# Layer norms centred early on the mean of their first half, and first units that begin with the high parts

## The chip, the cores and the metric

The kernel runs on one core of a Trainium2 chip. The metric is the device time of one launch in microseconds (us), as the median of several runs. All numbers of the profile come from one profiled execution.

## What is computed

The reference runs two transformer blocks after each other on one sequence of 256 tokens of width 1024, in fp32. The first block has two layers: sparse attention and gated linear attention as mixers, each followed by a layer norm, then a squared-relu MLP followed by a layer norm. These four norms are what the change is about:

```python
def layer_norm(x, g, b):
    xf = x.astype(jnp.float32)
    mu = jnp.mean(xf, axis=-1, keepdims=True)
    var = jnp.mean(jnp.square(xf - mu), axis=-1, keepdims=True)
    return ((xf - mu) * lax.rsqrt(var + LN_EPS) * g + b).astype(x.dtype)

# first_block, layer i
h = layer_norm(DN_ALPHA * h + mix, ln_mix_g[i], ln_mix_b[i])                          # ln0, ln2
h = layer_norm(DN_ALPHA * h + squared_relu_mlp(h, mlp_w_up[i], mlp_w_down[i]), ...)   # ln1, ln3
```

The second block normalises by rms (pre_mix, post_mix, pre_x, post_x, pre_ffn, post_ffn, mem), and has its own mixers, cross attention and a gated MLP.

## The kernel before

Activations stand transposed: 8 blocks of 128 features by 256 tokens, in `h` (the residual stream) and `z`. Weights are read as 183 "units" of 128 x 2048 elements, in one fixed order, by DMAs from the SP queue into four buffers `raw`. Each unit is split in two: ScalarE copies the high part to `whi` (`high_part`), VectorE subtracts to get the low part `wlo` (`low_part`). Both run three units ahead of the products (AHEAD = 3). Activations are split the same way into `xh` and `xl`, in four chunks of two blocks, with the semaphores `split_hi` and `split_lo`. A product of a unit is three matmuls (`three`): high by high, high weight by low activation, low weight by high activation. A unit is 48 matmuls of 128 x 256 into one of four PSUM banks `lin`. Each use of a bank is a "job" with a number; `plan()` writes out the order of the jobs by hand, TensorE follows it, and ScalarE and VectorE each have an order of their own, joined by semaphores only.

- Narrow units `ao` and `go` (4 each, before ln0 and ln2): each makes two blocks. VectorE's `residual` does for each: `low_part`, z = ALPHA * h + product (L1546), and two additions to `zsum` (`add_up`, L1538).
- Down units `dn` (8 for each half of an MLP): each makes one block. The second half adds to `z` (L1728) and to `zsum`. Up and down units run in loops of two times four.
- `layer_norm`: TensorE multiplies `zsum` by a matrix of ones (L580), so every partition has the sum over features. VectorE subtracts 1/1024 of it from `z` in four operations (`center`, L1461). ScalarE squares each chunk (L1023), VectorE adds the two blocks of chunks 2 and 3 (L1452), TensorE sums the squares over features (`token_sum`, L544), ScalarE takes the root (`deviation`, L1036), VectorE the inverse (L1454), TensorE spreads it over the partitions (`spread`, L567). VectorE scales (L1476), ScalarE makes `xh` (L1055), VectorE makes `xl` (L1490) and writes `h` (L1506).
- `unit_first` is the first unit after a norm: for each chunk it waits for `split_lo` and does all three kinds of product of that chunk, for both output blocks.
- `keep_warm(n)` puts n products of the identity with itself (L537) into TensorE's queue; nobody reads them. `norm` has 6 (or 0) of them before the square sum, 4 before the spreading and 11 after it, `layer_norm` has 5 before the mean.
- A product in full fp32 (L537, L544, L567, L580) is shown as two records in the profile.

Of the kernel before, what the change touches and what calls it, by code (L numbers as in the profile page):

```python
# [17 lines left out]
P = 128  # L18
S = 256
D = 1024  # L20
DB = D // P
RING = 4
# [45 lines left out]
def plan():  # L68
# [18 lines left out]

    add("ik"); units("iq", 2); add("iw"); add("rope", 0); add("rope", 1); add("rope", 2)
# [10 lines left out]
    units("ao", 4); norm("ln0", True)  # L99
    for layer in range(2):  # L100
        for half in range(2):
            units(f"up{layer}{half}", 8); units(f"dn{layer}{half}", 8)
        norm(f"ln{2 * layer + 1}", True)
        if layer == 0:
# [11 lines left out]
            units("go", 4); norm("ln2", True)  # L116
# [14 lines left out]
    for u in range(COUNT["fd"]):  # L131
# [11 lines left out]
          ("inv", 1), ("rot", 1), ("norot", 1), ("ln_eps", 1), ("rms_eps", 1), ("one", 1), ("zero", 1)]  # L143
# [6 lines left out]
def shape_constants():  # L150
# [32 lines left out]
    put("one", np.ones((P, 1)))  # L183
    return c

def build(nc, units_d, x_d, mem_d, pos_d, vec_d, const_d, narrow_a_d, narrow_b_d, narrow_f_d, w_a2_d, b_fgt_d, lam_d, out_d):
# [4 lines left out]
    with ctx:  # L192
# [36 lines left out]
        squares_of = pr + lg  # L229

# [65 lines left out]
        z_summed, centered, squared, normed = sem("z_summed"), sem("centered"), sem("squared"), sem("normed")  # L296
        paired, scaled, inv_ready = sem("paired"), sem("scaled"), sem("inv_ready")
# [23 lines left out]
        CENTERED = counts([(e, 3) for e in ("ln0", "ln1", "ln2", "ln3", "conv")])  # L321
        SQUARED = counts([("ln0", 4), ("ln1", 4), ("ln2", 4), ("ln3", 4), ("pre_mix", 4), ("conv", 2), ("mem", 4),
                          ("post_mix", 4), ("pre_x", 4), ("post_x", 4), ("pre_ffn", 4), ("post_ffn", 4)])

        PAIRS = {"ln0": (2, 3), "ln1": (2, 3), "ln2": (2, 3), "ln3": (2, 3), "conv": (0, 1), "mem": range(4), "post_mix": range(4),
# [5 lines left out]
        SUMMED = {"ln0": 0, "ln1": 8, "ln2": 16, "ln3": 24}  # L331
# [119 lines left out]
        def _(pe):  # L451
# [29 lines left out]
            def unit_first(u, j, event, g=None):  # L481
# [9 lines left out]
                last.then_inc(job_done, 1)  # L491

            def unit_down(u, j, first, g=None):
# [3 lines left out]
                for k in range(UT):  # L497
                    if first is not None and k % 2 == 0:
                        pe.wait_ge(flo, first + k // 2 + 1)
# [77 lines left out]
            def layer_norm(name):  # L577
# [3 lines left out]
                norm(name)  # L581
# [154 lines left out]
            ups("ao", "ao")  # L736
# [3 lines left out]
            def mlp(layer):  # L740
                for half in range(2):
# [7 lines left out]
                    with pe.Fori(0, 2) as g:  # L749
                        for i in range(RING):  # L750
# [1450 lines left out]
```

## Time and profile before

| | |
|---|---|
| runs | 1348.9, 1351.1, 1351.09 us; median 1351.09 |
| the profiled execution | 1351.66 us, its span 1349.9 us |
| TensorE matmul (PE) | 1295.1 us, 96% of the span |
| VectorE (DVE) | 899.4 us, 67% |
| ScalarE (ACT) | 643.9 us, 48% |
| chain that ended last | PE 78%, DVE 13%, ACT 3%, issue 3%, POOL 2%, DMA 1% |
| mean granted TensorE clock | 0.992 |

The busy share of PE is an upper bound on useful work: it contains the idle products of `keep_warm`, and matmuls overlap in the records. The chain of waits says for each moment what the end of the program hung on.

### The profile page before, as it was taken

Reading aid. Unit: us, or ns where it says so; the run is one execution under the profiler, and the core shown is the slowest. Engines: PE = TensorE matmul, PEld = TensorE weight load, DVE = VectorE, ACT = ScalarE, POOL = GpSimd, SP = SyncE. Lnnn points to the kernel's source line nnn. Section 1 sums busy time; section 2 is a strip of 40 time slices with the busy share of each in tenths; the row PEclk is TensorE's granted clock in tenths of the full one; section 3 lists DMA queues with packets and bytes.
Section 4 is the critical chain, followed back from the end, with each engine's and each line's share of the span. In section 5 each row is a group of like instructions: output and inputs, shape, how many; then the busy total and the mean of one; then the engine's idle time right before and its main releaser. Section 6 shows DMA issues by size and latency. Waiting matters only on the chain.

```text
span 1349.9 us, 25141 instructions
## 1 busy us (share of the span) xinstructions
PE 1295.1 (96%) x10650; PEld 1251.7 (93%) x10650; DVE 899.4 (67%) x1373; ACT 643.9 (48%) x838; POOL 46.3 (3%) x40
## 2 busy tenths in 40 slices
PE   9989999999997999999999999999799999999997
PEld 8869999999886999999999998889798989999997
DVE  6875764565568576556664369879766564899843
ACT  5463553543463435335345453544445455777631
POOL 0561000000000000000000000000000000000000
PEclk9999999999998999999999999999999999999999
DMA  9223355554332135555524543334355241455530
GB/s 363 97 95 103 112 192 187 181 193 156 128 125 80 56 117 187 190 184 187 187 70 186 183 161 100 120 126 142 139 179 196 94 157 63 142 176 183 185 126 32
DMA packets 28505, 198.41 MB, mean 147 GB/s; under 512 B 3440, under 2 KB 3952, under 8 KB 4736
## 3 DMA queue, kind: packets, MB, share of 16 engines
q1 hardware_dynamic: 27792, 195.83, 40.5%
q10 hardware_dynamic: 624, 1.31, 0.3%
q8 instruction: 66, 1.08, 0.3%
q14 instruction: 23, 0.19, 0.0%
HBM read 196.08 MB, written 1.05 MB: 146 GB/s over the span
## 4 chain that ended last, share of the span: by engine, by line
PE 78%; DVE 13%; ACT 3%; issue 3%; POOL 2%; DMA 1%; SPq 0%; DVEq 0%; ACTq 0%
PE lin L462 23%; PE lin L464 22%; PE lin L463 22%; DVE conv L1910 3%; DVE wlo L1436 3%; PE lin L544 3%; PE att L537 2%; ACT whi L997 1%; PE lin L567 1%; DMA narrow_a<-narrow_a_dram 1%; PE att L623 1%; POOL pr L447 1%; DVE qk L1777 1%; DVE z L1527 0%; POOL lg L447 0%
## 5 line engine op out<-in xcount | busy, mean ns | idle before, releaser
L462 PE MATMUL lin<-xh,whi 128*128 128x256 f32 x1936 | 555.7, 287 | 3.9 <-DVE xl L1490 2.1
L1436 DVE TENSOR_TENSOR wlo<-raw,whi 128x2048 fp32r<-128x2048 f32 x179 | 409.6, 2291 | 211.6 <-ACT whi L997 210.5
L463 PE MATMUL lin<-xl,whi 128*128 128x256 f32 x1936 | 549.7, 284 | 0.0
L464 PE MATMUL lin<-xh,wlo 128*128 128x256 f32 x1936 | 549.4, 284 | 0.0
L997 ACT ACTIVATE whi<-raw 128x2048 fp32r<-128x2048 f32 x183 | 348.5, 1906 | 180.4 <-PE lin L464 171.0
L462 PEld LDWEIGHTS lin<-xh,whi 128*128 128x128 f32 x1936 | 373.4, 193 | 9.1 <-issue 5.7
L463 PEld LDWEIGHTS lin<-xl,whi 128*128 128x128 f32 x1936 | 373.5, 193 | 0.6 <-issue 0.5
L464 PEld LDWEIGHTS lin<-xh,wlo 128*128 128x128 f32 x1936 | 373.2, 193 | 0.0
L462 PE MATMUL lin<-fh,whi 128*128 128x256 f32 x512 | 143.4, 280 | 0.0
L464 PE MATMUL lin<-fh,wlo 128*128 128x256 f32 x512 | 142.9, 279 | 0.0
L463 PE MATMUL lin<-fl,whi 128*128 128x256 f32 x512 | 142.9, 279 | 0.0
L464 PEld LDWEIGHTS lin<-fh,wlo 128*128 128x128 f32 x512 | 96.3, 188 | 0.0
L462 PEld LDWEIGHTS lin<-fh,whi 128*128 128x128 f32 x512 | 96.1, 188 | 0.0
L463 PEld LDWEIGHTS lin<-fl,whi 128*128 128x128 f32 x512 | 95.8, 187 | 0.0
L537 PE MATMUL att<-consts 128*128 128x128 f32 x512 | 64.5, 277 | 0.0
L537 PEld LDWEIGHTS att<-consts 128*128 128x128 f32 x512 | 60.6, 192 | 1.9 <-issue 1.7
L1910 DVE SCALAR_TENSOR_TENSOR conv<-upad,vec,conv 128x256 f32<-128x256 f32 x120 | 58.1, 484 | 3.9
L462 PE MATMUL lin<-whi,xh 128*128 128x256 f32 x176 | 50.5, 287 | 0.0
L463 PE MATMUL lin<-wlo,xh 128*128 128x256 f32 x176 | 49.8, 283 | 0.0
L464 PE MATMUL lin<-whi,xl 128*128 128x256 f32 x176 | 49.8, 283 | 0.0
L462 PE MATMUL lin<-gh,whi 128*128 128x256 f32 x176 | 49.3, 280 | 0.0
L464 PE MATMUL lin<-gh,wlo 128*128 128x256 f32 x176 | 49.1, 279 | 0.0
(335 smaller groups left out, 1621.3 us busy)
## 6 DMA issues: line engine op xcount, KB each, us to landing
raw<-units_dram SPq DMA_DIRECT2D x183, 1024.0 KB, 4.8
h<-x_dram SPq DMA_DIRECT2D x1, 1024.0 KB, 6.9
memT<-mem_dram ACTq DMA_DIRECT2D x1, 1024.0 KB, 4.8
out_dram<-h SPq DMA_DIRECT2D x4, 256.0 KB, 2.0
consts<-consts_dram SPq DMA_DIRECT2D x1, 864.0 KB, 15.5
narrow_a<-narrow_a_dram SPq DMA_DIRECT2D x1, 544.0 KB, 9.0
vec<-vectors_dram SPq DMA_DIRECT2D x1, 245.5 KB, 17.7
posi<-pos_dram SPq DMA_DIRECT2D x1, 128.0 KB, 8.8
```

The costliest lines, as they stand in the source:

```text
L447: last = nc.gpsimd.tensor_scalar(x, x, ainv[:, n, m:m + 1], None, ALU.mult)
L462: mm(out, w[0], a[0], start=first, stop=False)
L463: mm(out, w[0], a[1], start=False, stop=False)
L464: return mm(out, w[1], a[0], start=False, stop=last)
L537: mm(att[0][:, 0:P], ident, ident, start=True, stop=True)
L544: ins = mm(flat[:, (col + t) * width:(col + t + 1) * width], block[:, t * P:(t + 1) * P], ones[:, 0:width], start=first and t == 0, stop=l ...
L567: last = mm(o[:, n, t * P:(t + 1) * P], inv[:, col:col + 1].broadcast_to([P, P]), ident, start=True, stop=True)
L623: last = mm(o, v, pT[u % 2][:, n, :], start=b == 0, stop=b == att_keys(u, m) // P - 1)
L997: f(whi[u % RING][:], raw[u % RING][:], ACT.Copy).then_inc(hi_ready, 1)
L1436: v.tensor_tensor(wlo[u % RING][:], raw[u % RING][:], whi[u % RING][:].bitcast(f32), ALU.subtract).then_inc(lo_ready, 1)
L1777: ins = v.tensor_tensor(part[0], part[1], part[2], ALU.mult)
L1910: ins = v.scalar_tensor_tensor(out=conv[:, b, :], in0=x, scalar=w, in1=conv[:, b, :], op0=ALU.mult, op1=ALU.add)
```

## The change

- The job order gets a product `ln_shift` for each layer norm. It multiplies `zsum` by ones when only half of the blocks have been added, within unit 2 of `ao`/`go` or unit 4 of the last down units (`near_sum`).
- `near_shift` on VectorE then subtracts this mean (twice the half sum over 1024) from all eight blocks: from `z` where it is there, from `h` (divided by ALPHA) or the half-made `z` where the product is still to come. It corrects `zsum` by the same.
- ScalarE squares the shifted blocks as they come (`near_squares`), VectorE adds the squares block by block (`add_squares`).
- After the last block the product of `zsum` with ones gives the mean that is left. ScalarE squares one row of it (`shsq`), and TensorE adds -1 times this to the one remaining sum of squares. VectorE subtracts the mean left from `z` and then takes the inverse.
- The last narrow unit is written as two jobs of one block each (`two_jobs`). The second-half down units are written out instead of looped.
- `unit_first` does the products with the high activations of chunks 0 and 1 first, and those with the low ones one chunk later.
- Idle products: 2 instead of 4 before the spreading in every `norm`; in a layer norm 1 and 2 around the small product and 8 after the spreading.

```diff
@@ plan @@
+    def narrow_units(name, ln):
+        add(name, 0, name); add(name, 1, name); add(ln + "_shift"); add(name, 2, name); add(name, 3, name, 2)
+        norm(ln, True)
...
@@ tensor @@
-                for c in range(4):
+                def with_high(c):
+                    pe.wait_ge(split_hi, SPLIT[event] + c + 1)
+                    for m in range(2):
+                        for k in (2 * c, 2 * c + 1):
+                            w = tile(u, m * DB + k)
+                            mm(o[:, m, :], w[0], xh[:, k, :], start=m == k == 0, stop=False)
+                            mm(o[:, m, :], w[1], xh[:, k, :], start=False, stop=False)
+
+                def with_low(c):
                     have(event, c + 1)
                     for m in range(2):
                         for k in (2 * c, 2 * c + 1):
-                            last = three(o[:, m, :], tile(u, m * DB + k), (xh[:, k, :], xl[:, k, :]), m == k == 0, m == 1 and k == DB - 1)
+                            last = mm(o[:, m, :], tile(u, m * DB + k)[0], xl[:, k, :], start=False, stop=m == 1 and k == DB - 1)
+                    return last
+
+                with_high(0)
+                for c in range(1, 4):
+                    with_high(c)
+                    with_low(c - 1)
+                with_low(3).then_inc(job_done, 1)
...
+            def near_sum(ln):
+                pe.wait_ge(z_summed, SUMMED[ln] + 4)
+                mm(bank(JOB[ln + "_shift", 0])[:, 0, :], ones, zsum[:], start=True, stop=True).then_inc(job_done, 1)
...
             def norm(name, idle=6):
                 keep_warm(idle)
                 square_sum(name)
-                keep_warm(4)
+                keep_warm(2)
                 spread(name)
                 keep_warm(11)
...
                 mm(bank(JOB[name + "_mean", 0])[:, 0, :], ones, zsum[:], start=True, stop=True).then_inc(job_done, 1)
-                norm(name)
+                pe.wait_ge(near_added, ADDED[name] + 5)
+                o = bank(JOB[name + "_sq", 0])
+                token_sum(o, 0, squares_of[0][:, 0, :], True, False)
+                keep_warm(1)
+                pe.wait_ge(shift_squared, LN[name] + 1)
+                flat = o[:].rearrange("p a s -> p (a s)")
+                for t in range(2):
+                    last = mm(flat[:, t * P:t * P + 8], shsq[:, t * P:(t + 1) * P], const("neg")[0:1, :], start=False, stop=t == 1)
+                last.then_inc(job_done, 1)
+                keep_warm(2)
+                spread(name)
+                keep_warm(8)
...
@@ scalar @@
             def layer_norm(name, event, bias):
-                squares(name, z, is_centered(name))
+                j = JOB[name + "_mean", 0]
+                filled(act, j)
+                f(shsq, lin[j % RING][0:1, 0, :], ACT.Square, scale=D ** -0.5).then_inc(shift_squared, 1)
                 deviation(name, D, eps_ln)
...
@@ vector @@
-                center(name, z, D)
+                j = JOB[name + "_mean", 0]
+                p = psum(j)
+                dve.wait_ge(shift_squared, LN[name] + 1)
+                for c in range(4):
+                    ins = v.scalar_tensor_tensor(out=two(z, c), in0=over(p[:, 0, :]), scalar=-1.0 / D, in1=two(z, c), op0=ALU.mult, op1=ALU.add)
+                    if c == 3:
+                        read_out(ins, j)
+                    elif c == 2:
+                        link(ins)
                 inverse(name)
-                link(v.memset(zsum[:], 0.0))
-                is_centered(name)
+                evacuated(dve, j)
...
+            def near_shift(ln, src, alpha):
+                j = JOB[ln + "_shift", 0]
+                p = psum(j)
+                for n, c in enumerate((2, 3, 0, 1)):
+                    v.scalar_tensor_tensor(out=two(z, c), in0=over(p[:, 0, :]), scalar=-2.0 / D / (alpha if c >= 2 else 1.0),
+                                           in1=two(src if c >= 2 else z, c), op0=ALU.mult, op1=ALU.add).then_inc(shifted, 1)
+                read_out(v.scalar_tensor_tensor(out=zsum[:], in0=p[:, 0, :], scalar=-8.0 / D, in1=zsum[:], op0=ALU.mult, op1=ALU.add), j)
+                evacuated(dve, j)
+                dve.wait_ge(shifted, 4 * LN[ln] + 4)
...
+            def residual(name, ln):
+                sq = squares_of
                 for i in range(4):
                     low_part(U0[name] + i + AHEAD)
                     j = JOB[name, i]
+                    if i == 2:
+                        near_shift(ln, h, ALPHA)
+                    elif i == 3:
+                        add_squares(ln, 1, 2, sq[0][:], sq[1][:])
+                        add_squares(ln, 2, 3, sq[0][:], sq[2][:])
+                        add_squares(ln, 3, 3, sq[0][:, 0, :], sq[0][:, 1, :])
+                    if i < 3:
+                        ...
+                    else:
+                        for m in (6, 7):
+                            j = JOB[name, 3] + m - 6
+                            read_out(v.scalar_tensor_tensor(out=z[:, m, :], in0=z[:, m, :], scalar=ALPHA, in1=psum(j)[:, 0, :], op0=ALU.mult, op1=ALU.add), j)
+                            evacuated(dve, j)
+                            add_up(m, SUMMED[ln] + m + 1)
+                            add_squares(ln, 4 + m - 6, 4 + m - 6, sq[0][:, 0, :], sq[3][:, m - 6, :])
...
@@ vector, second-half down units @@
+                        ln, sq = f"ln{2 * layer + 1}", squares_of
+                        for i in range(8):
+                            low_part(U0[dn] + i + AHEAD)
                             j = JOB[dn, i]
+                            if i == 4:
+                                near_shift(ln, z, 1.0)
+                            elif i == 6:
+                                add_squares(ln, 1, 2, sq[0][:], sq[1][:])
+                            elif i == 7:
+                                add_squares(ln, 2, 4, sq[0][:], sq[2][:])
+                                add_squares(ln, 3, 5, sq[0][:, 0, :], sq[0][:, 1, :])
+                                add_squares(ln, 4, 5, sq[0][:, 0, :], sq[3][:, 0, :])
+                            read_out(v.tensor_tensor(z[:, i, :], z[:, i, :], psum(j)[:, 0, :], ALU.add), j)
+                            evacuated(dve, j)
+                            add_up(i, SUMMED[ln] + i + 1)
+                        add_squares(ln, 5, 6, sq[0][:, 0, :], sq[3][:, 1, :])
```

## Rows read from the trace of the kernel before

**Rows 1.** The page, part 1: busy us (share of the span) and instructions.
```profile
PE 1295.1 (96%) x10650; PEld 1251.7 (93%) x10650; DVE 899.4 (67%) x1373; ACT 643.9 (48%) x838; POOL 46.3 (3%) x40
```

**Rows 2.** The chain of waits around ln0: start us, length us, what.
```profile
134.05 0.70 DVE z L1546
...
135.72 0.71 PE lin L580 x2
...
142.42 0.88 DVE z L1476 x2
...
144.27 0.89 DVE xl L1490 x2
```

**Rows 3.** Timeline of VectorE, 128 to 155 us: start, length, engine, line, operation, count.
```profile
128.29 0.69 DVE L1546 SCALAR_TENSOR_TENSOR z<-h,lin 128x512 f32<-128x512 f32 x1 [1.39 <-PE lin L464]
129.01 0.89 DVE L1538 TENSOR_TENSOR zsum<-zsum,z 128x256 f32<-128x256 f32 x2
130.37 2.29 DVE L1436 TENSOR_TENSOR wlo<-raw,whi 128x2048 fp32r<-128x2048 f32 x1 [0.47 <-ACT whi L997]
...
136.52 2.48 DVE L1461 SCALAR_TENSOR_TENSOR z<-lin,z 128x512 f32<-128x512 f32 x4 [0.86 <-PE lin L580]
...
141.28 0.17 DVE L1454 RECIPROCAL inv<-dev 128x2 f32<-128x2 f32 x1 [1.15 <-ACT dev L1036]
...
148.49 0.88 DVE L1490 SCALAR_TENSOR_TENSOR xl<-z,vec,xh 128x256 fp32r<-128x256 f32 x2 [0.19 <-ACT xh L1055]
...
153.92 0.68 DVE L1715 TENSOR_TENSOR sqr<-relu 128x512 f32<-128x512 f32 x1
```

**Rows 4.** Timeline of ScalarE at ln0.
```profile
139.69 1.28 ACT L1036 ACT_TABLE_LOAD   x1
140.98 0.26 ACT L1036 ACTIVATE dev<-lin,consts 128x2 f32<-128x2 f32 x1
143.33 1.71 ACT L1055 ACTIVATE xh<-z,vec 128x256 fp32r<-128x256 f32 x4 [2.09 <-DVE z L1476]
...
147.55 0.91 ACT L1055 ACTIVATE xh<-z,vec 128x256 fp32r<-128x256 f32 x2 [0.67 <-DVE z L1476]
...
151.54 0.60 ACT L1167 ACTIVATE relu<-lin 128x512 f32<-128x512 f32 x1 [1.27 <-PE lin L464]
```

**Rows 5.** Timeline of TensorE: full fp32 products of 256 columns, and idle products.
```profile
11.95 3.65 PE L683 MATMUL lin<-h,narrow_a 128*72 128x256 f32 x16 [1.23 <-DMA narrow_a<-narrow_a_dram]
...
142.11 2.62 PE L537 MATMUL att<-consts 128*128 128x128 f32 x22
```

**Rows 6.** Timeline of VectorE at ln1: last residual, and inverse.
```profile
328.52 0.42 DVE L1728 TENSOR_TENSOR z<-z,lin 128x256 f32 x1 [1.53 <-PE lin L464]
...
334.94 0.17 DVE L1454 RECIPROCAL inv<-dev 128x2 f32<-128x2 f32 x1 [1.14 <-ACT dev L1036]
```

**Rows 7.** The chain of waits: idle products around pre_mix, the DMA of memT.
```profile
689.22 3.80 PE att L537 x34
...
697.93 2.46 PE att L537 x22
...
1030.09 4.80 DMA memT<-mem_dram
```

**Rows 8.** Waits of TensorE: us in total, times, longest.
```profile
PE lin L462 <- DVE xl L1446: 1.1, 3, 0.5
```

**Rows 9.** Timeline of TensorE: two starts after idle time, in brackets.
```profile
395.21 1.57 PE L785 MATMUL lin<-qk 128*64 128x64 f32 x32 [3.18 <-DVE qk L1777]
...
960.34 1.97 PE L905 MATMUL lin<-conv,consts 128*128 128x256 f32 x8 [2.91 <-DVE conv L1910]
```

**Rows 10.** Windows: busy us (x) by engine, granted clock, DMA share, GB/s.
```profile
396.00:397.00 1.00, 1.00 (x17) 0.88 (x14) 0.35 (x1) 0.61 (x1) 0.00 (x0) 0.50 1.01 418
...
420.00:430.00 10.00, 6.80 (x102) 6.50 (x103) 9.79 (x15) 4.77 (x4) 0.00 (x0) 0.51 0.22 93
...
961.00:962.00 1.00, 1.00 (x8) 0.87 (x6) 1.00 (x1) 0.00 (x0) 0.00 (x0) 1.00 0.00 0
```

More of the change, by code:

```diff
@@ L98, in plan @@
         add("scores", p, banks=2)
-    units("ao", 4); norm("ln0", True)
+    narrow_units("ao", "ln0")
     for layer in range(2):
         for half in range(2):
-            units(f"up{layer}{half}", 8); units(f"dn{layer}{half}", 8)
+            units(f"up{layer}{half}", 8)
+            if half == 0:
+                units(f"dn{layer}0", 8)
+        for i in range(8):
+            if i == 4:
+                add(f"ln{2 * layer + 1}_shift")
+            add(f"dn{layer}1", i, f"dn{layer}1")
         norm(f"ln{2 * layer + 1}", True)
@@ L115, in plan @@
             add("gla_sq"); add("gla_rstd", 0); add("gla_rstd", 1)
-            units("go", 4); norm("ln2", True)
+            narrow_units("go", "ln2")
     norm("pre_mix")
@@ L183, in shape_constants @@
     put("one", np.ones((P, 1)))
+    put("neg", -np.ones((P, 8)))
     return c
@@ L320, in build @@
         SCALED = counts([(e, 3) for e in ("ln0", "ln1", "ln2", "ln3", "pre_mix", "mem", "pre_x", "pre_ffn")])
-        CENTERED = counts([(e, 3) for e in ("ln0", "ln1", "ln2", "ln3", "conv")])
-        SQUARED = counts([("ln0", 4), ("ln1", 4), ("ln2", 4), ("ln3", 4), ("pre_mix", 4), ("conv", 2), ("mem", 4),
+        CENTERED = counts([("conv", 1)])
+        LN = {"ln0": 0, "ln1": 1, "ln2": 2, "ln3": 3}
+        SQUARED = counts([("pre_mix", 4), ("conv", 2), ("mem", 4),
                           ("post_mix", 4), ("pre_x", 4), ("post_x", 4), ("pre_ffn", 4), ("post_ffn", 4)])
-        PAIRS = {"ln0": (2, 3), "ln1": (2, 3), "ln2": (2, 3), "ln3": (2, 3), "conv": (0, 1), "mem": range(4), "post_mix": range(4),
+        PAIRS = {"conv": (0, 1), "mem": range(4), "post_mix": range(4),
                  "post_x": range(4), "post_ffn": range(4)}
@@ L330, in build @@
                                        "post_x", "pre_ffn", "post_ffn")])
-        SUMMED = {"ln0": 0, "ln1": 8, "ln2": 16, "ln3": 24}
+        SUMMED = {ln: 8 * i for ln, i in LN.items()}
+        NEAR = counts([("ln0", 5), ("ln1", 6), ("ln2", 5), ("ln3", 6)])
+        ADDED = {ln: 5 * i for ln, i in LN.items()}
         def per(n, g, step):
@@ L735, in _ @@
             keep_warm(9)
-            ups("ao", "ao")
+            narrow_units("ao", "ln0", "ao")
             layer_norm("ln0")
@@ L842, in _ @@
             keep_warm(9)
-            ups("go", "go")
+            narrow_units("go", "ln2", "go")
             layer_norm("ln2")
@@ L1508, in layer_norm @@
                         ins.then_inc(normed, 1)
+                link(v.memset(zsum[:], 0.0))
                 dve.wait_ge(normed, NORMED[name] + 4)
```

114 lines of the change are left out of this document (82 added, 32 removed).

## The prediction

> **What bounds the kernel now.** I read the page first: the matrix engine is busy for 96% of the span [rows 1], so time is lost only in the few stretches where it has no product to do. The chain of waits shows such a stretch at each of the four layer norms. In the first [rows 2] the last product unit ends at 134.05 us and the next unit's first product waits for the low part written from 144.27 to 145.16. All that lies between is work of a norm: residual and sum, the mean by a product with ones, centring, squares, their sum, root, inverse, spreading, scaling, splitting. The timelines of VectorE and ScalarE put each step in its place [rows 3, 4]. So the norm's chain sets the time there, and whatever is moved under the last units is free only as long as VectorE has room beside them. A busy digit for the matrix engine proves nothing in these stretches: idle products on the identity fill them.
>
> **The room.** A narrow unit (ao, go) lasts 134.05 - 128.29 = 5.76 us [rows 2, 3]. VectorE's share of one is residual 0.69, two sums 0.89, one low part 2.29 [rows 3]: 3.9 of 5.76. A down unit has half as wide a residual and one sum: about 3.15 of 5.65.
>
> **Added product.** The mean of the first half is one product of 256 columns in full precision. Sixteen records of that shape took 3.65 us [rows 5], two take 0.46. It stands within a unit that keeps the matrix engine busy, so it is on the path: +0.46 for each norm, 1.8 in all.
>
> **ln0 and ln2 (after ao and go).** I count from the end of unit 1, t = 0 (122.53 by the 5.76 pitch). Unit 1's residual and sums end at 1.6, its low part lies at 2.1 to 4.4. The shift waits for it. It is four operations like centring, 2.48 us for four [rows 3], and one of 256 columns (0.42, as a sum): 4.4 to 7.3. Unit 2 ends at 6.2, its residual and sums run from 7.4 to 9.0, so VectorE is already a microsecond late. The low part goes to 11.3, then come two additions of 512 (0.68 each by the row of sqr [rows 3]) and one of 256: 13.2. Unit 3 ends at 11.95, so what is late next is VectorE. Two half residuals, two sums and one addition of squares, 0.42 to 0.45 each, follow: the sum is ready at 15.6. ScalarE's squares of the early blocks start at 8.2, behind the high part, and are never last. Before, the mean product stood at 135.72, t = 13.2: it comes 2.4 us later. From there the new chain is short. Mean product to reader is 136.52 - 135.72 = 0.80 [rows 2, 3]; the square of one row of 256 on ScalarE is between 0.26 (two columns) and 0.49 (256 columns with a pointer bias, half of the two in 0.91) [rows 4], I take 0.40 as nearest to the latter; then VectorE corrects z in 2.48, and the inverse is queued behind that, although the root is ready sooner. Inverse at 15.6 + 0.8 + 0.4 + 0.05 + 2.5 = 19.4, against 141.28, which is 18.75. So this part of the change makes ln0 and ln2 later by 0.6 each, the added product included. It takes the squares and most of their sums off the path and puts VectorE's own queue in their place.
>
> The table load of ln0 (1.28 us, 139.69 to 140.97) lay under the square sum, and the root began 0.01 us after it [rows 4]. Now it comes after the square of the row: 16.8 + 1.28 + 0.26 = 18.4, still a microsecond before VectorE is free at 19.4, so it costs nothing. If the cover were gone it would cost up to 1.28, once: ln1, ln2 and ln3 need no load. The Trainium skill (ScalarE: Activation LUTs, "What ACT_TABLE_LOAD costs") counts some 1380 ns of draining beside the 1283 ns of the load; by that ln0 alone would be another 0.4 us later and the total below 0.4 smaller. This case's trace shows the load at that length and no drain behind it.
>
> **ln1 and ln3 (after the down units).** The shift falls into unit 4 of 8: low part until 4.1 after the end of unit 3, shift and sum until 7.1, where unit 4 ends at 6.1. One microsecond late, but unit 5 has the room to give it back. In unit 7 the low part ends 4.1 after unit 6, then 0.68 + 0.43 + 0.43 of additions: 5.8 against the unit's 5.65. From the end t = 0 of the last unit: residual at 0.15, sum ready at 1.05, mean product at 1.1 (before, some 0.97), row read at 1.9, squared by 2.3, corrected until 4.8, inverse at 4.8. The last block's square and its addition end at 1.6, and its two token sums and the two small products follow before 2.7: not last. Before, the inverse began at 334.94 - 328.52 = 6.4 [rows 6]. Gain 1.6, less the 0.46 of the added product: 1.15. The shorter fill before spreading (below) makes it 1.25 each.
>
> **High products lead.** Scaling starts at S = 142.42; ScalarE's first two high blocks end at S + 1.8 and S + 2.6, the fourth at S + 6.0 and the third one pitch of 1.58 earlier [rows 4]; the low part of the first ends at S + 2.74, that of the last at S + 6.95 [rows 2, 3]. Before, the first product stood at S + 2.88 and ScalarE read the unit at 151.54, S + 9.1 [rows 4]. Now: 16 products with high parts from S + 1.85 (eight for a block, the product spacing being 5.76 / 48 = 0.12; 1.92 for blocks 0 and 1 together), low ones of block 0 until S + 4.2, block 2 from S + 4.5, block 3 from S + 6.1 to 7.1, the last low products until S + 8.0, read at S + 8.35. Gain 0.75 where the unit waits for its parts: ln0, ln1, ln2. At the other first units the data or the fill is ahead of the products: after pre_mix, for one, 22 fill records are the step before it [rows 7], and the first high part is ready before they end. There it is worth nothing. Products waited for plain low parts 1.1 us in all [rows 8], 0.9 of it at "out"; behind "out" ScalarE's squares of memT wait for a DMA of 4.80 us from 1030.09 [rows 7] that does not come sooner, and the matrix engine waits for those, so I count nothing there; the other end is 0.8.
>
> **Fill.** One idle product is two records; 22 records take 2.62 us or less in a row, about 0.23 for each product [rows 5]. Three fewer after each layer norm matter only where they gate: between ln3 and pre_mix 34 records (3.80 us) stand on the chain before a square sum whose first squares are there sooner [rows 7]. Six records fewer give 0.67. With the 1.25 that is 1.9 for ln3; the squares of pre_mix shift with it. Two fewer products between square sum and spreading (0.45 of cover) uncover only what the inverse needs, some 0.1 at each of the eight norms that have it (ln0 to ln3 too).
>
> **Other edits at nothing.** The memset of zsum moves behind the eight operations on h, under the first unit. The down units of the second half are written out instead of looped: narrow units, which are written out too, keep the matrix engine just as full as the loops do [rows 1]. Low parts and raw loads are a microsecond later in units 2 and 3, but they are three units ahead; that cover is about 17 us.
>
> **The sum**, against the profiled execution (1351.66; its span is 1349.9 and 1.8 lies around it): ln0 and ln2 +0.6 - 0.1 - 0.75 = -0.25 each; ln1 -1.25 - 0.75 = -2.0; ln3 -1.9; pre_mix, post_x, pre_ffn, post_ffn together -0.4. Total -4.8: 1346.9. The runs' median is 1351.09, 0.6 below that execution, so I forecast 1346.3. What follows ln1 is partly bound by VectorE, but all of it starts from the norm and moves with it.
>
> **The rivals.**
> (a) VectorE is later at the down units' end than I count (each wait between dependent additions costs a few hundredths in the rows and could cost 0.2; an ACT square could come last). For it: the budget there is 0.15 us over. Against it: unit 5 and 6 have slack. Then ln1 and ln3 gain about 0.3 each less the product: the total is -2.4, 1348.7.
> (b) The matrix engine's clock falls. In ln0 and ln2 fill ends at t = 13.1, the engine idles until 15.6, works some 2 us, idles again 17.7 to 19.7. In this trace 3.18 us without work (to 395.21) were followed by a granted clock of 0.50, while 2.91 us (to 960.34) left it at 1.00 [rows 9, 10]. Each of the new gaps is shorter than either of those, but there are two close together, and no row shows that. The low level (1.2 GHz) after the former lasted about 3.3 us, and half of that is lost: 1.65 at each of two norms, -4.8 + 3.3 = -1.5, 1349.6. The Trainium skill (TensorE: Matmul & The Clock Gate, "HAM oscillation — how this bites in real kernels") warns of just such bursts between waits; the trace agrees for the longer gap and not for the shorter.
> (c) Slower than before: the same, but lasting. From 420 to 430 the clock stood at 0.51 for ten microseconds in which the engine also worked [rows 10]. If the low level reached through the first unit after ln0 and ln2, it would cost half of 9 us at each: -4.8 + 9 = +4.2, 1355.3. It decides from a loss of 7.5 us in all. Against it: whole first units follow at once.
> (d) The change does better: the correction's tail is hidden, the 0.8 of "out" passes: -6.5, 1344.6.
>
> **How the numbers follow.** Forecast 0.52 (1345.3 to 1348.3), (a) 0.13, (b) 0.15, (c) 0.10, (d) 0.10. A measurement of this kernel can tell about 0.2% (2.7 us) from no change, so faster means below 1348.4: forecast and (d), a little of (a): 0.63 in all (0.52 + 0.10 + 0.01). Within: the rest of (a) and most of (b), 0.26. Slower: (c) and a mix of (b) and (c), 0.11. The range leaves out (c) and the far end of (d): 1344.0 to 1351.0.
>
> **What would show it.** VectorE's timeline: after ao and go the product of zsum starts 3.7 us after unit 3 ends (1.7 before, [rows 2]); the inverse follows the fourth correction at once in all four norms. In ln1 and ln3 the inverse begins 4.8 us after the last down unit; if it is above 5.5, (a). The first product after a norm starts 1.85 us after scaling starts. The granted clock near 142 and 495: below 1.00 is (b). The forecast is wrong above all if the inverse does not wait for the correction, or if the two narrow norms lose more than 0.6 each.

## The result: slower, where a gain of 4.8 us was forecast

The changed kernel takes 1354.23 us (median of 12 runs, 1352.66 to 1355.36) beside 1351.10 for the kernel before (12 runs on the same chip). The ratio is 1.0026, with a 95% interval of 1.0017 to 1.0034: 3.1 to 3.5 us slower, and outside the range that was given (1344.0 to 1351.0). The profiled execution took 1354.28, its span is 1352.5 and its mean granted clock 0.985 (before: 0.992).

First the norms, since the forecast was about them. VectorE at ln0 after the change (start, length, engine, line, operation, count, idle time before), the counterpart of [rows 3]:

```profile
123.94 0.69 DVE L1689 SCALAR_TENSOR_TENSOR z<-h,lin 128x512 f32<-128x512 f32 x1 [1.39 <-PE lin L481]
...
128.23 1.28 DVE L1664 SCALAR_TENSOR_TENSOR z<-lin,h 128x512 f32<-128x512 f32 x2
129.42 1.28 DVE L1664 SCALAR_TENSOR_TENSOR z<-lin,z 128x512 f32<-128x512 f32 x2
130.62 0.41 DVE L1666 SCALAR_TENSOR_TENSOR zsum<-lin,zsum 128x256 f32<-128x256 f32 x1
...
138.71 0.42 DVE L1655 TENSOR_TENSOR zsum<-zsum,z 128x256 f32<-128x256 f32 x1
...
140.43 2.61 DVE L1606 SCALAR_TENSOR_TENSOR z<-lin,z 128x512 f32<-128x512 f32 x4 [0.77 <-ACT pT L1135]
142.96 0.16 DVE L1563 RECIPROCAL inv<-dev 128x2 f32<-128x2 f32 x1
144.00 1.66 DVE L1585 SCALAR_TENSOR_TENSOR z<-z,vec,lin 128x256 f32<-128x256 f32 x4 [0.89 <-PE lin L626]
```

The residual of unit 1 begins at 123.94. The shift (L1664), the late sum and the correction (L1606) stand in the order foretold, and the inverse (L1563) follows the correction with no idle time in brackets. It is 19.0 us behind 123.94; 19.4 was forecast from the unit's end. ScalarE and TensorE at the same norm, the counterparts of [rows 4, 2]:

```profile
139.93 0.37 ACT L1135 ACTIVATE pT<-lin 1x256 f32<-1x256 f32 x1 [0.80 <-PE lin L639]
140.32 1.28 ACT L1110 ACT_TABLE_LOAD   x1
141.61 0.26 ACT L1110 ACTIVATE dev<-lin,consts 128x2 f32<-128x2 f32 x1
...
152.31 0.60 ACT L1265 ACTIVATE relu<-lin 128x512 f32<-128x512 f32 x1 [0.46 <-PE lin L516]
```

```profile
139.19 0.70 PE L639 MATMUL lin<-zsum,consts 128*128 128x256 f32 x2 [2.23 <-DVE zsum L1655]
...
143.17 0.71 PE L626 MATMUL lin<-consts,inv 128*128 128x128 f32 x4 [1.34 <-DVE inv L1563]
143.72 1.95 PE L596 MATMUL att<-consts 128*128 128x128 f32 x16
145.96 0.36 PE L509 MATMUL lin<-xh,whi 128*128 128x256 f32 x1 [0.29 <-ACT xh L1141]
```

The table load ends at 141.60, the root begins at 141.61, and VectorE is not free before 142.96. The first product stands 1.96 us behind the start of scaling (forecast 1.85, before 2.88), the first unit is read 8.31 behind it (forecast 8.35, before 9.1). At ln1, beside [rows 6]:

```profile
331.46 0.42 DVE L1890 TENSOR_TENSOR z<-z,lin 128x256 f32<-128x256 f32 x1
...
336.16 0.15 DVE L1563 RECIPROCAL inv<-dev 128x2 f32<-128x2 f32 x1
337.54 1.66 DVE L1585 SCALAR_TENSOR_TENSOR z<-z,vec,lin 128x256 f32<-128x256 f32 x4 [1.22 <-PE lin L626]
```

The inverse comes 4.7 us behind the residual of the last unit instead of 6.4. So the norms did what they were meant to do. But that residual stood at 328.52 before [rows 6] and stands at 331.46 now: 2.9 us were lost ahead of ln1. The clock took 1.4 of them by a stretch at its lower level at 70 to 74 us, ahead of all changed code and behind a wait of 1.66 us that the kernel before has too (1.65, its clock stays at 1.00). The added products of ln0 and ln1 took 0.4 each, and the first unit after ln0 gave 0.9 back. The high parts of the down units show what else it was: some 1.6 us. ScalarE copies one for each unit, so two starts lie one unit apart where the matrix engine has no wait. Before, then after:

```profile
300.13 1.92 ACT L997 ACTIVATE whi<-raw 128x2048 fp32r<-128x2048 f32 x1 [3.74 <-PE lin L464]
305.79 1.92 ACT L997 ACTIVATE whi<-raw 128x2048 fp32r<-128x2048 f32 x1 [3.73 <-PE lin L464]
```

```profile
296.36 1.92 ACT L1071 ACTIVATE whi<-raw 128x2048 fp32r<-128x2048 f32 x1 [3.84 <-PE lin L481]
302.12 1.92 ACT L1071 ACTIVATE whi<-raw 128x2048 fp32r<-128x2048 f32 x1 [3.84 <-PE lin L481]
307.88 1.92 ACT L1071 ACTIVATE whi<-raw 128x2048 fp32r<-128x2048 f32 x1 [3.84 <-PE lin L481]
```

A down unit lasted 5.66 us and lasts 5.76, with the same 48 products, the clock at its upper level and no wait within it; the step is the same in the down units of the first half, whose code the change does not alter. 32 such units cost 32 x 0.105 = 3.4 us. The eleven longer units of the last feed-forward's second half (fd, which stream gh) lose 0.12 to 0.15 each, as 7.77 to 7.92, some 1.4 in all. That makes 4.8 us, as much as the norms were to give.

The second place is late in the program, where the matrix engine waits for the squares of memT (norm "mem", within the units of "out"). Before, then after, with the first full microsecond of products behind the wait:

```profile
1041.71 1.13 PE L544 MATMUL lin<-consts,pr 128*128 128x128 f32 x8 [1.98 <-DVE pr L1452]
1042.00:1043.00 1.00, 1.00 (x11) 1.00 (x10) 0.57 (x2) 0.00 (x0) 0.00 (x0) 1.00 0.66 115
```

```profile
1040.82 2.05 PE L603 MATMUL lin<-consts,pr 128*128 128x128 f32 x8 [3.09 <-DVE pr L1561]
1041.00:1042.00 1.00, 1.00 (x5) 1.00 (x6) 0.67 (x3) 0.00 (x0) 0.00 (x0) 0.50 0.45 98
```

In each pair the first line is from the timeline and the second from the windows. Up to there the profile of the changed kernel was ahead: the high part number 133 (the units are counted from 0) starts at 983.78 us against 985.07 before, in spite of the longer down units. Behind the longer wait its clock stands at 0.50 from 1040 to 1046, and the two steps between high parts that span the place take 15.66 us (1036.11 to 1051.77) instead of 13.01 (1037.01 to 1050.02): 2.65 us. The experiments take both places up.

### The profile page after: what moved, and what is told of

The parts are those of the page before. It is cut to its first block, busy times and chain, and to the rows that moved or that the text cites. A ratio compares the mean times of both kernels' runs of the same rounds, so it can differ in the third digit from the quotient of the medians.

```text
span 1352.5 us, 24795 instructions
## 1 busy us (share of the span) xinstructions
PE 1292.8 (96%) x10498; PEld 1247.5 (92%) x10498; DVE 917.0 (68%) x1407; ACT 644.3 (48%) x848; POOL 46.3 (3%) x40
## 4 chain that ended last, share of the span: by engine, by line
PE 79%; DVE 12%; ACT 3%; issue 3%; POOL 2%; DMA 1%; SPq 0%; DVEq 0%; ACTq 0%
PE lin L479 21%; PE lin L480 21%; PE lin L481 21%; DVE wlo L1545 2%; DVE conv L2071 2%; PE att L596 2%; PE lin L603 2%; PE lin L509 2%; PE lin L516 2%; PE lin L510 2%; ACT whi L1071 1%; PE lin L626 1%; PE att L693 1%; DVE z L1606 1%; DMA narrow_a<-narrow_a_dram 1%
## 5 line engine op out<-in xcount | busy, mean ns | idle before, releaser
L479 PE MATMUL lin<-xh,whi 128*128 128x256 f32 x1728 | 495.9, 287 | 0.8 <-POOL wlo L453 0.7
L480 PE MATMUL lin<-xl,whi 128*128 128x256 f32 x1728 | 490.9, 284 | 0.0
L481 PE MATMUL lin<-xh,wlo 128*128 128x256 f32 x1728 | 490.7, 284 | 0.0
L479 PEld LDWEIGHTS lin<-xh,whi 128*128 128x128 f32 x1728 | 334.0, 193 | 4.3 <-issue 2.8
L480 PEld LDWEIGHTS lin<-xl,whi 128*128 128x128 f32 x1728 | 334.0, 193 | 0.7 <-issue 0.5
L481 PEld LDWEIGHTS lin<-xh,wlo 128*128 128x128 f32 x1728 | 333.6, 193 | 0.0
L596 PE MATMUL att<-consts 128*128 128x128 f32 x416 | 56.7, 287 | 0.0
L596 PEld LDWEIGHTS att<-consts 128*128 128x128 f32 x416 | 52.2, 200 | 1.8 <-issue 1.7
L509 PE MATMUL lin<-xh,whi 128*128 128x256 f32 x208 | 52.9, 289 | 0.6 <-ACT xh L1141 0.6
L510 PE MATMUL lin<-xh,wlo 128*128 128x256 f32 x208 | 51.5, 283 | 0.0
```

Source lines behind the costliest of these rows:

```text
L479: mm(out, w[0], a[0], start=first, stop=False)
L480: mm(out, w[0], a[1], start=False, stop=False)
L481: return mm(out, w[1], a[0], start=False, stop=last)
L509: mm(o[:, m, :], w[0], xh[:, k, :], start=m == k == 0, stop=False)
L510: mm(o[:, m, :], w[1], xh[:, k, :], start=False, stop=False)
L596: mm(att[0][:, 0:P], ident, ident, start=True, stop=True)
```

## The experiments

```diff
-  ..., ("zero", 1), ("neg", 8)]
+  ..., ("zero", 1), ("neg", 1)]
...
-    put("neg", -np.ones((P, 8)))
+    put("neg", -np.ones((P, 1)))
...
-  last = mm(..., const("neg")[0:1, :], start=False, stop=t == 1)
+  last = mm(..., const("neg")[0:1, :].broadcast_to([1, 8]), start=False, stop=t == 1)
```

> The changed kernel with one edit: the constant of -1 takes one column instead of eight (read by a broadcast), so every buffer after the constants, fh, fl, gh and gl among them, has the address it had before the change (32 bytes lower). Theory L (the shift of 32 bytes slows the down products, 0.1177 to 0.120 us each over 32 down units and 11 units of the last product): 4 to 5 us faster than the changed kernel, so 1349 to 1350.5, ratio to before about 0.999. Theory C (the loss is the low clock after ln1 and ln3 alone): the down products stay at 0.120 us, the time stays at 1354, ratio 1.0025.

e2 and e3 are the kernel before with unused columns at the end of the constants.

```diff
-  ..., ("one", 1), ("zero", 1)]
+  ..., ("one", 1), ("zero", 1), ("pad", 8)]
```

> The kernel before with eight unused columns behind the constants, so that all buffers after them lie 32 bytes higher, as in the changed kernel; no instruction differs. Theory L: down products at 0.120 us, 4 to 5 us slower than before, ratio 1.003 to 1.004. Theory C: ratio 1.000.

> The kernel before with sixteen unused columns behind the constants: all buffers after them lie 64 bytes higher. If what counts is whether fh and fl start at a multiple of 64 bytes (before: yes, shifted by 32: no), ratio 1.000 and down products at 0.1177 us. If it counts that they are offset by 64 from a multiple of 128 (before: yes; here they are at a multiple of 128, as xh and xl are, whose products take 0.120 us), ratio 1.003 to 1.004. Theory C: ratio 1.000.

Measured: e1 1347.78 us, ratio 0.9979 (0.9971 to 0.9988). e2 1355.54, 1.0041 (1.0028 to 1.0054). e3, with 16 columns, 1354.67, 1.0027 (1.0018 to 1.0035). e1 came out 1.2 us below the range expected for it, e2 and e3 at most 0.0003 beside theirs. High parts of down units in e1, then e2, then e3:

```profile
294.33 1.92 ACT L1071 ACTIVATE whi<-raw 128x2048 fp32r<-128x2048 f32 x1 [3.73 <-PE lin L481]
299.99 1.92 ACT L1071 ACTIVATE whi<-raw 128x2048 fp32r<-128x2048 f32 x1 [3.74 <-PE lin L481]
305.64 1.92 ACT L1071 ACTIVATE whi<-raw 128x2048 fp32r<-128x2048 f32 x1 [3.73 <-PE lin L481]
```

```profile
295.76 1.92 ACT L997 ACTIVATE whi<-raw 128x2048 fp32r<-128x2048 f32 x1 [3.84 <-PE lin L464]
301.52 1.92 ACT L997 ACTIVATE whi<-raw 128x2048 fp32r<-128x2048 f32 x1 [3.84 <-PE lin L464]
```

```profile
294.95 1.92 ACT L997 ACTIVATE whi<-raw 128x2048 fp32r<-128x2048 f32 x1 [3.77 <-PE lin L464]
300.65 1.92 ACT L997 ACTIVATE whi<-raw 128x2048 fp32r<-128x2048 f32 x1 [3.78 <-PE lin L464]
```

e1 has 5.66 again and the changed kernel's gain comes to light: 3.3 us below before. e2 computes and issues exactly what the kernel before does, only 32 bytes of nothing are added, and it is 4.4 us slower with the changed kernel's 5.76. So the shift of addresses is a cause, shown from both sides. e3 (`fh` at 0) has 5.70, between the two; its units explain about 2 of its 3.6 us, and the rest has no row.

**2. Which address counts.** In the kernel before, units that stream xh (at 0, as the weights are) take 5.76, those that stream fh (at 64) 5.66. Either xh's own place is bad or its distance from the weights. e4 is the kernel before with 64 bytes ahead of xh, and 64 more ahead of consts, so that xh goes to 64 and the weights and fh stay at 0 and 64. e5 is e1 with the same. e11 leaves xh at 0 and fh at 64 and moves the weights to 64.

```diff
+  sbuf("pad0", [P, 16])
   xh = sbuf("xh", [P, DB, S], f32r)
   xl = sbuf("xl", [P, DB, S], f32r)
+  sbuf("pad1", [P, 16])
   consts = sbuf("consts", [P, NC])
```

> The kernel before with an unused 64 bytes ahead of xh and 64 more ahead of the constants: xh and xl are then offset by 64 from a multiple of 128, as fh and fl are in the kernel before, and stay so. If this offset is what makes the down products take 0.1177 us, the up and narrow products fall from 0.120 to 0.1177 us: some 5300 to 6300 products, 12 to 14 us faster, ratio 0.990. If the two spacings come from the kind of unit (up and down) and not from addresses, ratio 1.000.

> The changed kernel with the constant of -1 in one column and, besides, 64 unused bytes ahead of xh and 64 ahead of the constants: fh, fl, xh and xl all offset by 64 from a multiple of 128. If the gain of the edits (0.9979 with the old addresses) and the gain of the addresses (0.9851 in the kernel before) add up, ratio 0.983 and about 1328 us. If the shorter units leave VectorE less room beside ao and go, so that the sums end later after the last unit, one or two us of that are lost: 0.985.

> The kernel before with the weights' two parts whi and wlo offset by 64 bytes from a multiple of 128, xh, xl at a multiple and fh, fl offset by 64, as before. If the spacing of the products goes by the address of the streamed activations alone, nothing changes: up units 5.76 us, down units 5.65, ratio 1.000. If it goes by the distance between weights and activations, the two swap: up units 5.65 us and down units 5.76, ratio 0.990 to 0.993.

Measured: e4 1331.30 us (1326.35 to 1337.42), ratio 0.9851 (0.9828 to 0.9874). e5 1333.89, 0.9871 (0.9856 to 0.9886). e11 1340.39, 0.9917 (0.9903 to 0.9930). High parts of up units, which stream xh: before, e4, e11.

```profile
250.61 1.90 ACT L997 ACTIVATE whi<-raw 128x2048 fp32r<-128x2048 f32 x1
256.36 1.90 ACT L997 ACTIVATE whi<-raw 128x2048 fp32r<-128x2048 f32 x1
```

```profile
243.31 1.90 ACT L999 ACTIVATE whi<-raw 128x2048 fp32r<-128x2048 f32 x1
248.97 1.90 ACT L999 ACTIVATE whi<-raw 128x2048 fp32r<-128x2048 f32 x1
```

```profile
249.51 1.90 ACT L999 ACTIVATE whi<-raw 128x2048 fp32r<-128x2048 f32 x1
255.16 1.91 ACT L999 ACTIVATE whi<-raw 128x2048 fp32r<-128x2048 f32 x1
```

The length of a unit (mean of many starts, units with a wait or an added product left out) and the offsets modulo 128:

| kernel | weights | xh | up unit | fh | down unit |
|---|---|---|---|---|---|
| before, e1 | 0 | 0 | 5.76 | 64 | 5.655 |
| after, e2 | 0 | 0 | 5.76 | 96 | 5.76 |
| e3 | 0 | 0 | 5.76 | 0 | 5.70 |
| e4 | 0 | 64 | 5.653 | 64 | 5.655 |
| e11 | 64 | 0 | 5.654 | 64 | 5.695 |
| e5 | 0 | 64 | 5.654 | 64 | 5.44, some 5.65 |

e11 settles it: xh did not move, the weights did, and up units gain 0.107 us while down units, whose distance is now 0, go from 5.655 to 5.695, nearly e3's 5.70 (5.76 was expected). What counts is the distance between the weights and what is streamed against them: at 64 modulo 128 a product takes 0.1178 us (5.654 / 48), at 0 or 96 between 0.1187 and 0.120. That xh at distance 0 takes 0.120 and fh at distance 0 only 0.1187 is not explained. Nearly all of the 140 units that are neither down nor fd stream xh, and 140 x 0.107 = 15 us is an estimate of at most what that is worth: most of e4's gain, which is 20 us in the medians (12 to 14 were expected) and 16.7 in the profiles (1334.97 against 1351.66).

The gains do not add up in e5. It was expected at 1328 us, or 1330 with a small loss; it is 1333.89, no faster than e4 without the change. Why the change's 3.3 us of e1 are not seen there stays open.

One row does not fit: most of e5's down units last 5.44 with e4's addresses. These are its high parts in down units of the first half:

```profile
202.19 1.92 ACT L1073 ACTIVATE whi<-raw 128x2048 fp32r<-128x2048 f32 x1 [3.52 <-PE lin L483]
207.63 1.92 ACT L1073 ACTIVATE whi<-raw 128x2048 fp32r<-128x2048 f32 x1 [3.52 <-PE lin L483]
```

It is 0.1133 us for a product. Counted by steps of 5.44 in the profiles, e5 has 24 such units, e12 15, e10 7, e4 4 and e11 2, not down units alone, and the nine kernels whose up units take 5.76 have none. So a further, quicker pace occurs where the distance at xh is 64, but the offsets don't decide which units get it: e4's down units have none of it, e10's within one execution have both. In all five down groups in which the pace had stood up to the unit with the added product of a layer norm (e5 and e12 two each, e10 one), the units behind that product are back at 5.65. The pace may be why e4's runs lie up to 11 us apart at the same mean clock (0.989 to 0.991), and why e5's profiled execution (1327.02) is 6.4 us below its next: 24 units by 0.215 are 5.2. That is argued, not shown.

**3. The two halves of the change, each alone.** e6 is the kernel before with high products leading in a norm's first unit. e9 is e1 without that.

```diff
+  with_high(0)
+  for c in range(1, 4):
+      with_high(c)
+      with_low(c - 1)
+  with_low(3).then_inc(job_done, 1)
```

> The kernel before with one part of the change: the first unit after a norm does its high products first. By the prediction's working 0.75 us at ln0, ln1 and ln2, nothing at the others, so 2.2 us faster, 1348.9, ratio 0.9984. If the waits at the first units are passed on to other waits, ratio 1.000 (then the gain measured with the old addresses is the norms' own).

> The changed kernel with the old addresses and the old order in the first unit after a norm: the norms' part alone. By the prediction's working ln0 and ln2 +0.5, ln1 -1.25, ln3 -1.9, the other norms -0.4: 2.5 us faster than before, 1348.5, ratio 0.9981. If the gain of the changed kernel with the old addresses (0.9979) is mostly the order of the first unit (0.9985 alone), ratio 0.9995.

Measured: e6 1348.65 us, 0.9985 (0.9976 to 0.9994); e9 1348.21, 0.9983 (0.9974 to 0.9992). In time each half is worth what the prediction put on it: leading 3 x 0.75 = 2.25 us (measured 2 to 2.5), the norms with the shorter fill 4.8 - 2.25 = 2.55 (measured 2.3 to 2.9). Together in e1 they give 3.3 and not 4.8.

For leading that agreement is partly luck. e6's high parts show the gains forecast, 0.71, 0.81 and 0.70 us at the first units after ln0, ln1 and ln2. But in "mem" e6 loses 2.55 us (the two steps take 15.56 instead of 13.01), and it gains some 3 us between 850 and 985 us, where the falls of the clock come and go from profile to profile. The loss in "mem" has its cause in the leading: the wait for the squares of memT is 1.97 to 2.17 us in the six kernels without it (before, e2, e3, e4, e9, e11) and 2.98 to 3.41 in the eight with it. The matrix engine is ready for them a microsecond sooner, and they come no sooner. By itself this costs nothing: e8, with 2.98, takes 13.00. But the clock fell behind it in four of the eight (after, e1, e6, e7; 1.4 to 2.8 us) and in none of the six.

**4. The clock.** The granted clock fell in norms after all. In the changed kernel's own profile it was not where rival (b) had it, at ln0 and ln2, but in its relatives it mostly was: of the twelve such norms of the changed kernel, e1, e5, e7, e9 and e10 it fell in nine. In the changed kernel's profile at ln1 (windows of 1 us; busy time of PE, PEld, DVE, ACT and POOL, granted clock, DMA share, GB/s):

```profile
336.00:337.00 1.00, 0.63 (x4) 0.63 (x4) 0.32 (x2) 0.00 (x0) 0.00 (x0) 0.80 0.00 0
337.00:338.00 1.00, 1.00 (x6) 1.00 (x6) 0.46 (x2) 0.00 (x0) 0.00 (x0) 0.50 0.00 0
...
142.00:143.00 1.00, 0.00 (x0) 0.00 (x0) 0.97 (x3) 0.00 (x0) 0.00 (x0) 1.00 0.00 0
```

It fell at ln1 and, likewise, at ln3 (0.50 from 689 to 691), each time behind an idle time of only 1.34 to 1.35 us; the longer gap of ln0 (2.23 us) left it at 1.00. In e1 it is the other way: 1.00 at ln0, ln1 and ln3, and 0.50 at ln2:

```profile
489.00:490.00 1.00, 1.00 (x6) 0.95 (x5) 0.00 (x0) 0.37 (x1) 0.00 (x0) 0.50 0.05 16
```

What such a fall costs, ln1 shows: VectorE waits 1.22 us for the spread inverse where e1 waits 0.88, and the first unit is read 8.75 us behind the start of scaling (346.29 - 337.54) where e1 has 8.29 (342.93 - 334.64), so 0.8 us on the path. The step between the two high parts on either side of a norm shows the rest (an asterisk where the clock fell within it; the one of ln3 takes in pre_mix):

| | before | after | e1 | e7 | e8 |
|---|---|---|---|---|---|
| ln0 | 20.01 | 19.76 | 19.76 | 20.52* | 19.76 |
| ln1 | 19.81 | 18.04* | 17.70 | 16.84 | 17.71 |
| ln2 | 20.01 | 19.76 | 20.53* | 19.93* | 19.75 |
| ln3 | 26.95 | 26.20* | 24.58 | 23.27 | 24.58 |

A fall costs 0.8 us at ln2 (e1 beside e8) and 1.5 at ln3 (after beside e1, less 0.1 for the unit's spacing). To take the falls away, e8 is e1 with enough idle products ahead of both waits.

```diff
-  keep_warm(5)
+  keep_warm(16 if name in ("ln0", "ln2") else 5)
   pe.wait_ge(z_summed, SUMMED[name] + DB)
...
-  keep_warm(2)
+  keep_warm(7)
   spread(name)
```

> The changed kernel with the old addresses and idle products where the matrix engine sat idle in a norm: 16 instead of 5 before the product of zsum in ln0 and ln2, 7 instead of 2 before the spreading in all four. Theory C (low clock in the norms): the granted clock stays at 1.00 through all four norms, and where one of them fell to 0.50 1.7 us come back for each fall; from one or two falls in a run, 1345 to 1347, ratio 0.996 to 0.997. If the fill itself gets in the way of the products, or the falls cost nothing, 0.998 or above.

Measured: 1347.62 us, 0.9975 (0.9965 to 0.9986), with e1 at 1347.78. The clock stands at 1.00 in all four norms (ln0, ln1, ln2, ln3):

```profile
133.00:146.00 13.00, 12.48 (x103) 11.77 (x102) 10.72 (x24) 4.46 (x9) 0.00 (x0) 1.00 0.23 83
333.00:340.00 7.00, 6.48 (x52) 6.14 (x52) 5.91 (x16) 3.39 (x8) 0.00 (x0) 1.00 0.00 0
486.00:498.00 12.00, 11.49 (x92) 10.65 (x91) 9.82 (x24) 4.08 (x10) 0.00 (x0) 1.00 0.18 72
684.00:692.00 8.00, 7.80 (x69) 7.61 (x69) 5.85 (x18) 3.57 (x9) 0.00 (x0) 1.00 0.01 3
```

And the time is the same. By the table the fill costs nothing at ln0, ln1 and ln3 and gives 0.8 back at ln2; e8's profile also has no fall in "mem" and gains 1.4 there, but 1.6 us are lost again between the high parts 131 and 133. The medians show no gain from the fill. They also show that falls in norms are not what makes the changed kernel 6.4 us slower than e1, which has one itself. Elsewhere each execution has low stretches of its own, the kernel before too (419 to 430, for one). In e1 the one in "mem":

```profile
1035.00:1036.00 1.00, 0.50 (x2) 0.53 (x3) 1.00 (x5) 0.00 (x0) 0.00 (x0) 0.50 0.00 0
```

Between the high parts 133 and 143 of e1, around that row, 1.5 us of what it was ahead of the kernel before are given back (from 6.4 to 4.8).

**5. The inverse ahead of half the correction.** In the changed kernel the inverse waits for four corrections, though the root is there sooner (141.87 of 142.96 at ln0). e7 is e1 with the inverse behind the second.

```diff
   for c in range(4):
       ins = v.scalar_tensor_tensor(...)
       if c == 3:
           read_out(ins, j)
       elif c == 2:
           link(ins)
-  inverse(name)
+      elif c == 1:
+          inverse(name)
```

> The changed kernel with the old addresses, and the inverse taken between the second and the third correction of z instead of behind all four. If VectorE's queue holds the inverse back (the root is ready 1.5 us before it in the changed kernel), the inverse begins 1.2 us sooner in all four norms; the scaling cannot start before the corrections end, so some 0.8 us of it arrive at each: 3.2 us faster than the 1347.8 of the changed kernel with the old addresses, ratio 0.9955. If the spreading is not what scaling waits for, ratio 0.998.

Measured: 1342.59 us, 0.9942 (0.9929 to 0.9956), 5.2 us below e1 where 3.2 were expected. VectorE at ln1:

```profile
331.56 1.29 DVE L1606 SCALAR_TENSOR_TENSOR z<-lin,z 128x512 f32<-128x512 f32 x2 [0.78 <-ACT pT L1135]
332.77 0.15 DVE L1563 RECIPROCAL inv<-dev 128x2 f32<-128x2 f32 x1
332.84 1.40 DVE L1606 SCALAR_TENSOR_TENSOR z<-lin,z 128x512 f32<-128x512 f32 x2
334.27 1.66 DVE L1585 SCALAR_TENSOR_TENSOR z<-z,vec,lin 128x256 f32<-128x256 f32 x4
```

The spreading now runs beside the other two corrections, and scaling follows them with no idle time. By the table above that saves 0.9 us at ln1 and 1.3 at ln3, where the clock fell in neither kernel, and 0.6 at ln2, where it fell in both; at ln0 it fell in e7 alone, and e7 is 0.8 slower there. These rows make 2.0 us, with the rest of the profile 1.3 (1345.18 against 1346.47, one of e7's slower executions); the 5.2 of the medians has no full account.

**6. All of it.** e10 is e5 with the inverse of e7, e12 is e10 with the fill of e8.

> The changed kernel with the constant of -1 in one column, xh and xl offset by 64 bytes, and the inverse between the second and third correction. If the three gains add up (0.9979 and 5 us of the inverse, 0.9851 of the addresses): 1323 to 1329 us, ratio 0.981. If what is gained by the inverse is lost at waits further on: as with the addresses alone, 0.987.

> The kernel of e10_best with the idle products of e8_fill in it (16 instead of 5 before the product of zsum in ln0 and ln2, 7 instead of 2 before the spreading). If falls of the clock in the norms cost time, 1.7 us for each fall less than e10_best, ratio 0.979 against 0.981. If not, or if five products more stand before a spreading that is now ready 1.2 us sooner, as e10_best or up to 1 us slower at each norm.

Measured: e10 1324.76 us (1321.22 to 1328.13), 0.9803 (0.9785 to 0.9821); e12 1327.82, 0.9834 (0.9821 to 0.9848). e10 is 26 us below before and 29 below the changed kernel. The fill costs 3 us in the median here (the two intervals touch at 0.9821) and brings nothing: the steps across ln1 and ln3 are 0.4 and 0.8 us longer in e12 than in e10, since five idle products now stand ahead of a spreading that is ready sooner.

## Why the prediction was wrong

**The step that failed** is "Other edits at nothing". It went through the memset, the unrolled units and the late low parts, but not the line that adds `neg`. An edit with no instruction was taken to have no time. It costs 4.4 us by e2, and up to 6.4 by e1 against the changed kernel: the new offset between fh and the weights. The spacing by unit accounts for 4.8 of these 6.4. Forecast -4.8 and offset +4.8 would give zero; the measured +3.1 is that, the 1.5 by which the gain was short in e1, and a rest of 1.6 between e1 and the changed kernel. Their two profiles, 7.8 us apart, differ beside the spacing by falls of the clock: the changed kernel loses 1.5 at 70 to 74 us, 1.5 at ln3, 0.7 at ln1 and 1.3 in "mem", e1 0.8 at ln2 and 0.8 at 403 to 411 us. How much of the 1.6 between the medians these are, no run says.

**A second step** is "I count nothing there", of the waits behind "out". It saw rightly that memT's DMA does not come sooner. What it left out is that the leading brings the matrix engine to that wait a microsecond sooner, and what the clock does behind a longer wait: 1.98 us became 3.09, and the profile loses 2.65 us.

**Added product.** 0.46 was right: the down unit with it lasts 6.19 (high parts at 307.88 and 314.07), 0.43 more than its neighbours.

**ln0 and ln2.** The inverse at 19.4 came at 19.0, less than half a microsecond off. The correction took 2.61, not 2.48, and the square of the row 0.37, not 0.40. The mechanism, VectorE's queue in place of the squares, is in the rows.

**Table load.** It stayed hidden, as forecast. The Trainium skill (ScalarE: Activation LUTs, "What ACT_TABLE_LOAD costs") counts a drain of some 1380 ns beside the load. The trace does not agree where it could be seen: the root starts 0.01 us behind the load, and with a drain between them it could not have begun before the inverse did. Nor does one lie ahead: 0.02 us pass between the end of the square (140.30) and the load (140.32).

**ln1 and ln3.** Inverse 4.8 us behind the unit forecast, 4.7 measured. In e1's profile the high parts show gains of 2.9 at ln1 and 2.6 at ln3, each less 0.43 for the added product: 2.5 and 2.2 beside the forecast 2.0 and 1.9.

**High products lead.** 1.85 and 8.35 behind scaling forecast, 1.96 and 8.31 measured; alone 0.9985 against 3 x 0.75 = 2.25 us, which is 0.9983. At ln0, ln1 and ln2 the mechanism is in the rows; that the whole came out the same took the luck told in experiment 3.

**Rivals.** (a) did not happen: the inverse was not late. (b) did not happen at ln0 and ln2 of the changed kernel, where it was forecast, but at ln1 and ln3; over its relatives it was right on the place too (nine of twelve), and put the price at twice what it is, 1.65 us forecast and 0.8 measured. The Trainium skill (TensorE: Matmul & The Clock Gate, "HAM oscillation — how this bites in real kernels") tells of bursts of some 2 us between waits of 3 to 5 us, each burst beginning at the low clock. The trace agrees in "mem" of the changed kernel (3.09 us). It does not where the clock stood (3.19 us in "mem" of e10) or fell behind less (1.34 us at ln1). (c) forecast slower by a lasting low clock through the first units; the kernel is slower, but 340 to 346 stands at 1.00 in its trace, no first unit after a layer norm but ln1's began low, and e8 without any fall in a norm keeps e1's time. The longest fall of the changed kernel is of (c)'s kind and was elsewhere, in "mem". None of the five cases held the main cause. The chance of 0.11 for slower had been worked out from the clock alone.

**What stays open:** what makes a down unit take 5.44 in some stretches and 5.65 in others at the same offsets; why fh at distance 0 is quicker than xh at distance 0; why e1's gain is 1.5 us short of the sum of its halves (the fall in "mem" gives 1.5 back in its profile, but e6 has that fall too); why the change brings nothing in e5; what decides whether the clock falls behind one and the same wait; and what else slows e3.

## What to carry to other kernels

Price a new buffer or constant, not only new instructions: add up which later buffers it moves, and modulo what. Before believing that a change does not pay, run it once with the old addresses, and run the old kernel once with the new ones; the two runs cost little and here turned a loss of 0.26% into a gain of 0.21%. Then read the length of unchanged work in the trace ahead of the place that was changed: if it differs, the cause isn't where the change was made. Read it behind the change as well: work that is ready sooner can end in a longer wait for something that isn't.

## What the runs showed of the hardware

The spacing of products of 256 fp32r columns with a weight load each depends on the byte distance, modulo 128, between the weights and the streamed activations: 0.1178 us at 64, 0.120 at 96, 0.1187 to 0.120 at 0. For this kernel the wrong distance at xh cost 17 us in the profiles and 20 in the medians (e4), of 1351, more than the whole change was meant to bring. The records of single products are no help: each shows 0.28 us in either case, and only the distance of their starts tells. A pace of 0.1133 exists too, in some stretches of the five kernels whose xh lies at 64 from the weights. And the granted clock fell behind 1.34 us without work (after, ln1), where it stood after 2.91 [rows 9] and after 3.19 (e10, "mem"): the length of the one gap doesn't decide, and the place of the falls changes from kernel to kernel.
